# Attention in head pairs with its steps between the projections, small loads moved, and the overflow branch placed earlier

## What is computed

```python
s = jnp.einsum('gpq,bcqgd->bcpgd', w, vc) + b_s...          # layer 0: spatial gating
mix = u * s
mo = memory_attention(qm, mk, mv)                            # softmax(q k / sqrt(64)) v
att = jnp.concatenate([mix, mo], -1) @ w_out_a[a]
...
s = jnp.where(valid, q @ kband * ATT_SCALE + bias, -inf)     # layer 1, one of three dilations
o = (exp(s - m) / l) @ vband;  mixed over dilations by softmax of the log-sums
...
sc = einsum(q, k) * 64 ** -0.5;  sc = where(col_mask, sc + bias, -inf)   # neighbourhood
x = x + (g_ret * y_ret + g_na * y_na + g_xa * y_xa) @ w_out
expert_block: (silu(xblk @ w_gate[e]) * (xblk @ w_up[e])) @ w_down[e]
```

## Time and profile before

| | |
|---|---|
| time, three runs | 1962.62 us median, 1954.67 to 1963.38 |
| profiled execution | 1962.68 us |
| span, first to last instruction | 1960.9 us |
| TensorE | 1821.7 us busy (93%) |
| VectorE, ScalarE | 289.1 us (15%), 242.9 us (12%) |
| mean granted TensorE clock | 0.964 |
| from device memory | 597.08 MB |

### The profile page before, as it was taken

How to read it: one execution, slowest core, us unless ns; L and a number is a source line. 1 busy time by engine, 2 the same in 40 slices (tenths; PEclk the granted TensorE clock), 3 DMA queues, 4 the chain that set the end, 5 groups by cost and what they waited for, 6 DMA issues and landing times.

```text
span 1960.9 us, 19208 instructions
## 1 busy us (share of the span) xinstructions
PE 1821.7 (93%) x8287; PEld 908.2 (46%) x8287; DVE 289.1 (15%) x817; ACT 242.9 (12%) x514; POOL 54.5 (3%) x78
## 2 busy tenths in 40 slices
PE   7999998998979899999989989899999999899997
PEld 4655332332323767633332323254654454655553
DVE  0232000000000123410000000031024031200001
ACT  1101100000000013110000000021121110111111
POOL 2000000000000000310000000000000000000000
PEclk8989999999999895999999999999999999799999
DMA  9628999999999630799999999992414432499992
GB/s 338 233 83 310 422 421 421 421 421 421 421 420 409 229 129 22 208 422 421 421 421 421 421 421 420 420 374 97 172 43 139 161 114 101 170 410 413 412 412 93
DMA packets 124950, 599.59 MB, mean 306 GB/s; under 512 B 9268, under 2 KB 18192, under 8 KB 71600
## 3 DMA queue, kind: packets, MB, share of 16 engines
q1 hardware_dynamic: 121104, 586.30, 74.6%
q0 software_dynamic: 3744, 11.86, 2.1%
HBM read 597.08 MB, written 1.05 MB: 305 GB/s over the span
## 4 chain that ended last, share of the span: by engine, by line
PE 44%; DMA 33%; issue 20%; DVE 2%; SPq 1%; ACT 0%; POOL 0%; POOLq 0%; DVEq 0%
DMA ring<-in_w_up_dram 32%; PE psum L343 22%; PE psum L504 12%; PE psum L421 2%; PE psum L399 2%; DMA ring<-in_w_in_a_dram 1%; PE psum L410 1%; PE psum L492 1%; PE psum L338 1%; PE psum L531 1%; PE psum L398 0%; PE psum L472 0%; PE psum L798 0%; SPq L1689 0%; PE psum L540 0%
## 5 line engine op out<-in xcount | busy, mean ns | idle before, releaser
L504 PE MATMUL psum<-ring,xT 128*64 128x512 f32 (+1 forms) x3072 | 590.7, 530 | 38.4 <-DMA ring<-in_w_up_dram 21.3
L504 PEld LDWEIGHTS psum<-ring,xT 128*64 128x64 f32 x3072 | 210.8, 138 | 366.9 <-issue 266.4
L504 PE MATMUL psum<-ring,work 128*64 128x512 f32 x1280 | 298.9, 601 | 35.3 <-DMA ring<-in_w_down_dram 33.1
L343 PE MATMUL psum<-ring,xT 128*128 128x512 f32 (+1 forms) x768 | 316.4, 573 | 11.5 <-DMA ring<-in_w_in_a_dram 7.7
L343 PEld LDWEIGHTS psum<-ring,xT 128*128 128x128 f32 x768 | 147.2, 193 | 175.3 <-issue 167.4
L504 PEld LDWEIGHTS psum<-ring,work 128*64 128x64 f32 x1280 | 86.7, 137 | 234.9 <-issue 144.0
L1344 DVE TENSOR_TENSOR work<-work,psum 128x512 f32<-128x512 f32 (+1 forms) x48 | 28.8, 599 | 942.3 <-PE psum L504 942.3
L492 PEld LDWEIGHTS psum<-work,x 128*128 128x128 f32 x768 | 95.2, 199 | 36.1 <-issue 36.1
L492 PE MATMUL psum<-work,x 128*128 128x128 f32 x768 | 103.7, 290 | 4.3 <-DVE work L1317 4.3
L835 ACT ACTIVATE work<-psum 128x512 f32<-128x512 f32 (+2 forms) x107 | 53.2, 504 | 402.3 <-PE psum L343 338.1
L343 PE MATMUL psum<-xT,ring 128*128 128x256 f32 x448 | 99.8, 385 | 1.5 <-issue 0.7
(11 more groups left out here) (197 smaller groups left out, 890.7 us busy)
## 6 DMA issues: line engine op xcount, KB each, us to landing
ring<-in_w_gate_dram SPq DMA_DIRECT2D x128, 1024.0 KB, 26.0
ring<-in_w_up_dram SPq DMA_DIRECT2D x128, 1024.0 KB, 24.5
ring<-in_w_down_dram SPq DMA_DIRECT2D x128, 1024.0 KB, 26.5
ring<-in_w_in_dram SPq DMA_DIRECT2D x16, 2048.0 KB, 8.2
ring<-in_w_exp_gate_dram SPq DMA_DIRECT2D x32, 1024.0 KB, 8.2
ring<-in_w_exp_up_dram SPq DMA_DIRECT2D x32, 1024.0 KB, 7.9
ring<-in_w_exp_down_dram SPq DMA_DIRECT2D x32, 1024.0 KB, 9.4
ring<-in_w_in_a_dram SPq DMA_DIRECT2D x3, 2048.0 KB, 25.2
```

Of the source, the lines that this page charges most:

```text
L343: ins = pe.matmul(b[:, cols_at[0]:cols_at[1]], lhsT=lhsT(c), rhs=rhs(c), start=(c == 0), stop=(c == k - 1))
L504: ins = pe.matmul(to[half * CAP:(half + 1) * CAP, 0:n], lhsT=lhsT, rhs=w[:, half * n:(half + 1) * n], start=first, stop=last)
```

## The change

The attention becomes a class with tasks in pairs of heads (rows 0 to 63 and 64 to 127 of the array). Weights are normalised before they are transposed (`normal`, VectorE), the output comes out transposed (`values`: v is the stationary operand, two heads into the two partition halves of one bank), and no `turn` of the output is left except for the retention. The signs of q and `flip` are turned so that the reduction is a minimum that ScalarE can use as bias directly; one VectorE instruction per task goes. All of the attention's steps stand between projections, in an order written out by hand. In A the mixing's output is also made transposed, `sg_b` comes by 12 broadcast loads, and the turn before the output projection goes. `...` marks what is cut.

```diff
-LAST = 2
+LAST = (5, 5, 2)
-        stream_0 = [[w_mem_k, w_mem_v], [w_in_a SGW], [w_in_a SGW+512], ...
+        stream_0 = [[w_mem_k, w_mem_v], [w_in_a SGW+512], [w_in_a SGW], ...
...
+            def scores(A, n, q, keys, bias=None):
+                t, heads = A.pairs[n]
+                for first in range(0, A.sources, A.together(n)):
+                    ...
+                    for g in range(first, min(A.sources, first + A.together(n))):
+                        o = [b[:, (g - first) * width:(g - first + 1) * width] for b in banks]
+                        if bias is not None:
+                            for a_ in range(2):
+                                pe.matmul(o[a_], lhsT=flip, rhs=bias(heads[a_], t), start=True, stop=False)
+                        last = [pe.matmul(o[a_], lhsT=q(heads[a_], t, g), rhs=keys(heads[a_], g)[:, 0:width], ...)
+                                for a_ in range(2)]
+            def turn_weights(A, n):
+                pe.wait_ge(S("att_w"), A.task(n, 1) + 1)
+                ...
+            def values(A, n, v):
+                pe.wait_ge(S("att_pT_a"), max(A.upto[n], A.upto[n + 1]))
+                b = bank("v", by=(S("att_o"), A.out(n)))
+                for m in (n, n + 1):
+                    ...
+                    for k, a_ in steps:
+                        o = b[a_ * HD:(a_ + 1) * HD, t * P:(t + 1) * P] if A.dv == HD else ...
+                        ins = pe.matmul(o, lhsT=v(...), rhs=pT[:, a_ * tiles + k, :], ...)
...
# expert_layer on TensorE (the other engines keep the order of If and Else)
+                early = N_EXP - LAST[k]
+                if k < DEPTH:
+                    with pe.If(fills > CAP):
+                        ...
+                    with pe.Else():
+                        ...
+                else:
+                    with pe.If(fills <= CAP):
+                        extras[k].skip(pe, "used gathered t_full pick_turned")
+                        experts(ph, None, early, N_EXP, closing=True)
+                    with pe.Else():
+                        ...
...
# stage A on TensorE
-            pe.wait_ge(S("con_in"), 16)
             pe.wait_ge(S("x_in"), 16)
+            two_turned(w[:, :, 256:512], xT, DC, 0, "a", "qm")
+            freed[n] = nat(w[:, :, 0:256], xT, DC, 256, "a", "gv", pack=True); n += 1
+            scores(att_0, 0, q, keys)
+            tile(w, xT, DC, 512, 0, "a", "gv")
+            scores(att_0, 1, q, keys)
+            turn_weights(att_0, 0)
+            freed[n] = tile(w, xT, DC, 512, 1, "a", "gv"); n += 1
+            scores(att_0, 2, q, keys)
+            turn_weights(att_0, 1)
+            two_turned(w, xT, DC, 0, "a", "u")
+            scores(att_0, 3, q, keys)
+            values(att_0, 0, v)
+            turn_weights(att_0, 2)
+            freed[n] = two_turned(w, xT, DC, 1, "a", "u"); n += 1
+            turn_weights(att_0, 3)
+            freed[n] = two_turned(as_cols(n, 0, 256), xT, DC, 0, "a", "u"); n += 1
+            values(att_0, 2, v)
...
# stage B: memory attention between q and k, then the dilated one between the last parts
+            two_turned(as_cols(n, 0, 256), xT, DC, 0, "a", "qkv")
+            values(att_m, 2, v)
+            wait_made("qkv")
+            scores(att_d, 0, dil_q, dil_k)
+            freed[n] = nat(as_cols(n, 2048, 256), xT, DC, 256, "a", "qkv", pack=True); n += 1
+            scores(att_d, 1, dil_q, dil_k)
+            turn_weights(att_d, 0)
+            tile(w, xT, DC, 512, 0, "a", "qkv")
+            scores(att_d, 2, dil_q, dil_k)
+            turn_weights(att_d, 1)
+            freed[n] = tile(w, xT, DC, 512, 1, "a", "qkv"); n += 1
+            scores(att_d, 3, dil_q, dil_k)
+            turn_weights(att_d, 2)
+            wait_made("qkv")
+            values(att_d, 0, dil_v)
+            turn_weights(att_d, 3)
+            values(att_d, 2, dil_v)
+            pe.wait_ge(S("att_o"), att_d.out(2))
...
# stage C: four cross-attention pairs between the gate tiles, eight neighbourhood pairs
# between the second halves of q and k, v, four gate tiles and the retention's q
+            scores(att_x, 0, xa_q, xa_k)
+            tile(w, xT, DC, 512, 0, "a", "gate")
+            scores(att_x, 1, xa_q, xa_k)
+            turn_weights(att_x, 0)
...
# ScalarE
+            def weights(A, n):
+                for a_ in range(2):
+                    act.wait_ge(S("att_nm"), I + 1)
+                    act.activation(p, src, ACT.Exp, bias=att_mx[:, I:I + 1], scale=-1.0, accum_out=...)
+            empty(gv[:, :, 512:SGW], "gv", ACT.Gelu)
+            weights(att_0, 0)
+            empty(gv[:, 0, 0:512], "gv", ACT.Gelu)
+            weights(att_0, 1)
+            turn_weights(att_0, 0)
...
# VectorE
+            def normal(A, n):
+                for a_ in range(2):
+                    dve.wait_ge(S("att_p"), I + 1)
+                    step(dve.reciprocal(att_rec[:, I:I + 1], att_sum[:, I:I + 1]))
+                    dve.tensor_scalar(p, p, att_rec[:, I:I + 1], None, ALU.mult).then_inc(S("att_w"), 1)
...
+                for g in range(2):      # the mixing in A, for each of three banks
+                    m = xT[:, tl, :]
+                    step(dve.tensor_tensor(..., bs[...], ALU.add))
+                    dve.tensor_tensor(m, m, u[:, tl, :], ALU.mult).then_inc(S("mix"), 1)
...
# GpSimd
-            pool.wait_ge(S("first_v_in"), 16)
+            pool.wait_ge(S("slot1"), landed[1])
             load(0)
+            for hh in range(N_SG):
+                pool.dma_start(W(L0["bs"], 6, P)[...], a["sg_b"][0][hh, :].partition_broadcast(HD))...
+            pool.dma_start(wr[:], ...)
-            pool.wait_ge(S("att_o"), 3 * TC * MEM_HEADS)
+            pool.wait_ge(S("att_o"), att_d.out(2))
             pool.dma_start(W(W_MEM2, TC, D), a["mem_2"][0]...)
+            pool.dma_start(W(W_AB, W_N - W_AB), a["later"]).then_inc(S("later_in"), 16)
...
# SyncE
                     if k == 0 and m == 0:
+                        sp.dma_start(x[:], ...)
+                    if k == 0 and m == 1:
                         sp.dma_start(con[:, P:], ...)
-                        sp.dma_start(x[:], ...)
                         sp.dma_start(W(L0["sgw"], N_SG, P), ...)
```

852 lines of the change are left out of this document (488 added, 364 removed).

## The result

| | before | after |
|---|---|---|
| median of the runs, us | 1959.2 (1954.7 to 1963.4, 4 runs) | **1885.9** (1882.7 to 1887.5, 4 runs) |
| ratio to before, 95% interval | 1 | 0.9624 (0.9594 to 0.9655) |
| profiled execution, us (span) | 1962.7 (1960.9) | 1882.7 (1881.0) |
| mean granted clock | 0.964 | 0.983 |

The forecast was 1892.7, the range 1878 to 1919. The two profiled executions lie 79.9 us apart, more than the medians (73.3), since the one of before was a long one and the one of after the shortest. Stage by stage, in us. A runs from the start to the first gather of layer 0 (the matmuls that pick an expert's tokens); an expert layer from its first gather to the start of its last scatter (the matmuls that bring an expert's output back to its tokens); B and C from there to the next first gather. "Again" is a second profile of the changed kernel, unchanged, from a later experiment.

What follows compares the result with a forecast made beforehand. TensorE's own order bounds A, B and C, the weights' DMA the experts. Gains 21.5 (A) + 33.3 (B) + 11 (C) + 7.2 (branches) - 3 = 70 us off 1962.7 give 1892.7 us, range 1878 to 1919.

Steps and rivals of the forecast that it cites:

- Start, 10.0: Start of A: chunk 1 issued earlier, 7.0 us of idle time and 3.0 of half-clock records gained; bounds 7 and 11.
- Attention and mixing in A, 11.5: A, sg_w transposes to z: attention in four head pairs gains 9.5 us, mixing without its turn 2.0.
- rival (1): Clock falls again between the last parts of A and B, costing 15 to 20 us: 1911 us; chance 0.12.
- B, 33.3: B: paired, interleaved attention takes 26 us instead of 59.0, gaining 33 (bounds 26 and 37); earlier turn of x nets 0.3.
- The mem_2 path: Behind B's attention: mem_2's load and VectorE's norm of x wait for its end; turn of x 17.2 us after z, not 18.5.
- C, 11: C: output turns gone 3.5 us, neighbourhood pairs at 2.8 us give 7.6, cross attention 0.0; bounds 5 and 15.
- Layer 0, 3.5: Layer 0's overflow branch: five experts behind it make up its stalls at 4 us each, gaining 3.5 us; bounds 0 and 5.3.
- Last layer, 3.2: Last layer's overflow branch: TensorE's usual case follows in order, so the 3.2 us gap goes; bounds 0 and 4.6.
- (2): Array halves don't overlap for short records and each part waits for its weights: 23 us more, 1916 us; chance 0.07.
- (3): VectorE and ScalarE take 2 to 3 us longer per pair than a projection part in 20 steps: 1943 us; chance 0.06.
- (4): Slower than before: inserted short steps pull the clock down for projections around them; at half of them 1993 us; chance 0.03.
- The -3 for mode changes and entries: Whole sum: 3 us taken off for tiling-mode changes of score and value groups and entries of the inserted steps.

Runs made afterwards that it cites:

- the one that recovered: Kernel before with only the branches' part (branch five experts from the end in layers 0 and 1, fall-through in the last layer): 1954.1 us, ratio 0.9963.
- the two last kernels: Changed kernel with z's first tile taking inputs as they become ready: 1876.3 us; that kernel with mem_2 also loaded earlier: 1871.6 us.
- the branch late: Changed kernel with the overflow branch two experts from the end in all three layers, the last layer's fall-through kept: 1883.5 us, ratio 0.9614.
- the doubled reductions: Changed kernel with the reduction over each head's scores done twice on VectorE, in every attention: 1887.8 us, ratio 0.9657.

## Why the prediction was right, and where it wasn't

- **What bounds the kernel.** It held: the experts of layers 0 and 1 took 465 to 470 us in every profile of every kernel, and nearly all the gain lies in A, B and C (73.4 of 79.9 us).
- **Start, 10.0.** The mechanism is shown by undoing it; 7.5 by the medians, 7.7 to 10.9 by the profiles. The wait is now 0.73, as forecast (0.75). The forecast stands at the upper end of what was measured, and no run tells the shares of its two moves.
- **Attention and mixing in A, 11.5.** z starts at 90.5 to 92.7 in the profiles of this order, forecast near 92. What was missed is the clock behind the new 3.3 us wait (0.83, worth 1.7 us). In the old order A's attention ran at half the clock too (0.50 from about 95 to 105 us), which the gain has in it. The prediction put the 6.8 us of VectorE's mixing into the sum as a duration and didn't ask what TensorE's clock does in them. That is rival (1) at a small size: it didn't come between the parts, but behind the wait. A second slow place lies behind the router's records: a projection took 8.84 us instead of 7.15 both in A and in B of after. The kernel before has it too (8.80 and 8.84), so it belongs to no wait that is new.
- **B, 33.3; measured 37.7.** The mechanism held, and it rests on the slow attention of the profile that the sum was taken against; against the one that recovered (170.5) the gain would be 22.7. From the first projection to z are 94.4 us. Before, they were 130.4, of which 59.0 were attention and 71.4 projections; so attention now adds 23.0, where the forecast had 26. The pieces that it priced came out: a wide and a narrow dilated score group 1.49 and 0.86 by the starts of successive rows (2.35 forecast), 36 values 2.19 (0.061 a record, forecast 0.065). The terms that failed are those set aside for what no row showed: "0.5 for the first scores' fourth bank" and "1 of entries" were nothing, and the last waits are 1.8, not 2.9. So the failed step is these reserves, 26 where 23.0 was measured. Ahead of the first projection another 0.5 was won, behind z 1.2.
- **The mem_2 path.** The turn of x 17.2 us after z was forecast and measured (716.60 to 733.84), and it was shown to be the bound there by the two last kernels.
- **C, 11; measured 14.8.** The neighbourhood's pair at 2.6 instead of 2.8 gives 9.3 instead of 7.6. The turns gave their 3.5, by the forecast's own rows. The term put at nothing, the cross attention, gave 1.3: its 8 tasks took 10.1 us in a row before (its first waits for weights included) and 8.9 between the parts. These make 14.1; the 0.73 us that TensorE stood idle ahead of the neighbourhood's first scores before, and no longer does, make up the rest.
- **Layer 0, 3.5; measured 3.2: a right number for a wrong reason**, and not a firm one, since the second profile of after has 1.3. The rate "4 us of a stall are made up per expert" came out (25.8 us an expert instead of 29.8). The failed step is that the place of the branch would give the 3.5: the prediction took both stalls of the kernel before as staying, 5.21 and 3.17, and three more experts behind them as the gain. In the changed kernel only the first is there, and two experts make it up (466.4 with the branch late, 466.3 with it early). What went away is the second stall, and why is open.
- **Last layer, 3.2; measured 4.8.** The step was right (a jump on the usual path, made up by nothing). The Trainium skill, "Runtime: NRT & Kernel Launch", Instruction fetch mechanics, says that a taken branch whose target lies outside the prefetched window has to wait for the fetch. The traces agree as far as they go: every jump in front of ready work has an idle time without a releaser there, 3.1 to 5.6 us; that it is the fetch, none of them shows. But the slow records behind it, which stood as the bound of 4.6, are part of the price in some programs: the term was mis-sized by them.
- **Rivals.** The halves overlap for scores and partly for values, so (2) fell (its own sum is a little low: 200 value records at 0.07 more are 14 us, not 12); (3) fell with the doubled reductions; (4) fell: in both profiles of after every window of an interleaved part stands at 0.99 or 1.00.
- **The -3 for mode changes and entries.** The profiles differ by 9.9 us more than forecast (79.9 against 70), and this term is 3 of them: it was kept for changes of mode beyond the prices, and the rows show score groups at 0.63 with the change of form in them and nothing more between the parts. By the medians the gain is 73.3, so the total (1885.9 for 1892.7) came nearer than the stages of the two profiles did. The Trainium skill, "TensorEngine Tiling (Array Packing)", Key Properties, says that changing the tiling mode drains the engine. The rows fit, with about 0.2 us a group (0.63 where 0.41 is the rate), and don't show the drain itself.

## What to carry to other kernels

Short dependent work of one stage belongs between the long independent parts of another, one long part behind each step that another engine must answer; here the order alone was worth 16 us, and up to 1.8 us more of VectorE's time in each dilated pair cost 1. Where a wait is left, let the consumer take its inputs in the order in which they become ready: it takes away the wait (3.3 us here) and may keep the clock up (1.7 more). A branch costs on the side that jumps, be it into a body or out of it, so look at what is behind both ends before choosing the one that falls through.

## What the runs showed of the hardware, not expected

- A jump on TensorE leaves it idle for 3.1 to 3.2 us in the last layer and 5.0 to 5.6 in the first two, in layer 0 of both kernels with the old attention even twice in a row (5.2 and 3.2, 5.3 and 3.3); behind it the next 16 records run at full speed in one kernel (1.95 us) and slowly in two others (3.31, 3.49).
- A body that falls through pays at its end: 4.34 us in the one kernel where TensorE has ready work there.
- For value chains of 64 columns in different halves the order hardly matters when each is two records long (4.4 and 4.6 us for 64); with six in a row it does (2.19 and 3.11 us for 36).
- After TensorE's wait of 3.3 to 3.7 us ahead of z in A the clock was 0.66 to 0.83 in the window behind it in nine of ten profiles and 1.00 in the tenth; after the jump of 3.08 us in the last layer it was 1.00, after one of 3.07 in another kernel 0.83. With the wait in pieces it stayed at 1.00 in both profiles. In stretches where the clock falls, the place differs from profile to profile by some 3 us of time.
